# One unit later: where the compressed keys' scores, softmax and turn stand in the first attention

## The reference

```python
sc = jnp.einsum('bgrqd,bgnd->bgrqn', qq, kc_h).astype(jnp.float32) * scale
valid = cmp_end[None, :] <= t[:, None]
p_c = jax.nn.softmax(jnp.where(valid, sc, NEG), axis=-1) * valid
o_c = jnp.einsum('bgrqn,bgnd->bgrqd', p_c.astype(vc_h.dtype), vc_h)
...
p_s = jax.nn.softmax(ss, axis=-1).reshape(b, g_n, r_n, QUERY_BLOCK, top, SEL_BLOCK)
o_s = jnp.einsum('bgrqkc,bgqkcd->bgrqd', p_s.astype(v_sel.dtype), v_sel)
...
p_w = jax.nn.softmax(jnp.where(m_w, sw, NEG), axis=-1)
o_w = jnp.einsum('bgrqk,bgkd->bgrqd', p_w.astype(vwb.dtype), vwb)
return gg[..., 0:1] * o_c + gg[..., 1:2] * o_s + gg[..., 2:3] * o_w
```

## Time and profile before

| what | us |
|---|---|
| median of 3 runs | 1531.16 (1530.28 to 1531.87) |
| the profiled execution's own time | 1531.69 |
| its span | 1529.9 |
| PE busy in the span | 1505.9 (98%) |
| DVE busy | 1203.9 (79%) |
| ACT busy | 1015.9 (66%) |
| chain that ended last: PE's share | 81% |

### The profile page before, as it was taken

How to read it: one execution, slowest core, us unless ns; L and a number is a source line. 1 busy time by engine, 2 the same in 40 slices (tenths; PEclk the granted TensorE clock), 3 DMA queues, 4 the chain that set the end, 5 groups by cost and what they waited for, 6 DMA issues and landing times.

```text
span 1529.9 us, 29802 instructions
## 1 busy us (share of the span) xinstructions
PE 1505.9 (98%) x12684; PEld 1400.1 (92%) x12684; DVE 1203.9 (79%) x1702; ACT 1015.9 (66%) x1566; POOL 8.3 (1%) x18
## 2 busy tenths in 40 slices
PE   9999999999999999999999999999999998999998
PEld 9999999988889999999988889969999897899997
DVE  7999766889758799667898768876898578688864
ACT  7786865667646776765676546685777467677753
POOL 0000000000000000000000000000000001000000
PEclk9999999999999999999999999999999999999999
DMA  7522135555554422244655546402555543255551
GB/s 291 193 95 102 57 138 193 205 183 193 207 178 158 158 98 85 84 165 166 233 191 184 214 170 241 165 1 87 218 193 193 191 142 136 84 208 182 191 193 55
DMA packets 35700, 245.55 MB, mean 161 GB/s; under 512 B 4208, under 2 KB 4592, under 8 KB 6512
## 3 DMA queue, kind: packets, MB, share of 16 engines
q1 hardware_dynamic: 35568, 243.65, 44.5%
HBM read 242.58 MB, written 1.05 MB: 159 GB/s over the span
## 4 chain that ended last, share of the span: by engine, by line
PE 81%; DVE 11%; ACT 5%; DMA 1%; issue 1%; SPq 0%; DVEq 0%; ACTq 0%
PE PS L420 81%; DVE WL L1982 2%; DVE SB L1991 1%; DVE SB L1982 1%; DVE SA L1982 1%; ACT SB L1232 1%; DMA RAW<-w_in 1%; ACT WH L1235 1%; ACT SB L1909 1%; DVE SB L2260 1%; DVE SB L1986 1%; ACT SB L1235 1%; PE PS L423 0%; DVE SA L1991 0%; DVE SA L2162 0%
## 5 line engine op out<-in xcount | busy, mean ns | idle before, releaser
L420 PE MATMUL PS<-XHL,WH 128*128 128x256 f32 (+2 forms) x4080 | 847.9, 301 | 4.6 <-ACT SA L1410 2.8
L420 PEld LDWEIGHTS PS<-XHL,WH 128*128 128x128 f32 (+1 forms) x4080 | 645.8, 187 | 41.4 <-issue 5.9
L420 PE MATMUL PS<-XHL,WL 128*128 128x256 f32 (+1 forms) x2392 | 670.0, 280 | 0.0
L1235 ACT CAST WH<-RAW 128x2048 fp32r<-128x2048 f32 (+1 forms) x235 | 427.3, 1822 | 267.3 <-PE PS L420 255.4
L1982 DVE TENSOR_TENSOR WL<-RAW,WH 128x2048 fp32r<-128x2048 f32 (+1 forms) x235 | 512.0, 2181 | 109.2 <-ACT WH L1235 108.8
L420 PEld LDWEIGHTS PS<-XHL,WL 128*128 128x128 f32 (+1 forms) x2392 | 448.8, 188 | 0.4
L420 PE MATMUL PS<-INHL,WH 128*128 128x512 f32 (+1 forms) x1216 | 334.2, 343 | 0.0
L420 PE MATMUL PS<-INHL,WL 128*128 128x256 f32 x960 | 270.0, 281 | 0.0
L420 PEld LDWEIGHTS PS<-INHL,WH 128*128 128x128 f32 x1216 | 210.1, 188 | 27.6
L420 PEld LDWEIGHTS PS<-INHL,WL 128*128 128x128 f32 x960 | 181.2, 189 | 0.0
L1982 DVE TENSOR_TENSOR SB<-SB 128x510 f32<-128x510 f32 (+3 forms) x171 | 112.6, 660 | 14.8 <-ACT SB L1232 11.4
(11 more groups left out here) (156 smaller groups left out, 1436.7 us busy)
## 6 DMA issues: line engine op xcount, KB each, us to landing
RAW<-w_in SPq DMA_DIRECT2D x51, 1024.0 KB, 4.8
RAW<-w_up SPq DMA_DIRECT2D x44, 1024.0 KB, 4.8
RAW<-f_in SPq DMA_DIRECT2D x44, 1024.0 KB, 4.8
RAW<-w_down SPq DMA_DIRECT2D x22, 1024.0 KB, 4.8
RAW<-f_out SPq DMA_DIRECT2D x22, 1024.0 KB, 4.8
RAW<-a_w_in SPq DMA_DIRECT2D x10, 1024.0 KB, 4.9
RAW<-w_out SPq DMA_DIRECT2D x8, 1024.0 KB, 4.7
RAW<-w_bdn SPq DMA_DIRECT2D x4, 1024.0 KB, 4.8
```

The source lines that it names most:

```text
L420: return e.matmul(out, l, r, start=start, stop=stop, skip_group_check=True)
L1235: e.copy(out, x).then_inc(*A.up(*key, of=of))
```

## The change

In all three engines one number goes up by one. `cmp_scores` moves from u = 1 to u = 2, behind the second value chunk and ahead of `turn(0)`. DVE's `cmp_soft` and ACT's exponential move from u = 2 to u = 3, `cmp_turn` and the copy from u = 3 to u = 4. `compressed(0)` stays at the end of `av(1)` at u = 4. No instruction is added or taken away. The banks of PSUM are handed out in another order, since the compressed scores take theirs later.

```diff
@@ tensor @@
                             ps.give(st, "v", u - 1)
-                        if u == 1:
+                        if u == 2:
                             cmp_scores()
                     if 0 <= u - 2 < 16:
                         turn(u - 2)
-                    if u == 3:
+                    if u == 4:
                         cmp_turn()
                     if u < 16:
                         for r in range(2):
                             ps.give(st, "sc", u, r)
-                        if u == 2:
+                        if u == 3:
                             ps.give(st, "cs")
```

## The result

The changed kernel takes 1535.72 us (median of 8 runs, 1535.18 to 1536.76), the kernel before in the same comparison 1531.45 (8 runs, 1530.05 to 1534.05). The ratio is 1.0028, with a 95% interval of 1.0019 to 1.0038: 4.3 us slower. The forecast was 1534.0 with a range of 1532.0 to 1536.3.

What follows compares the result with a forecast made beforehand. PE, busy 98% of the span, was taken as the bound. 1531.69 + 1.6 (new waits of 4.7 less 2.8 removed, within 0.3) + 1.0 for the clock gave 1534.3, adjusted towards the median to 1534.0; range 1532.0 to 1536.3.

Steps and rivals of the forecast that it cites:

- forecast case: New PE waits for DVE plus a clock fall: 1534.0 us, own range 1533.0 to 1535.7, chance 0.55.
- The value chunk at the full clock: Second value chunk, now behind dense matmuls, runs at 2.4 GHz: 5.78 us in place of 6.89, 1.11 less.
- running clock: Step-by-step timeline from 982.16 with lengths from before, putting scores(5) at 1004.1, 1.6 us later than before.
- The waits that go: PE's 0.79 us wait inside turn(1), for values(1), and a mask's 0.47 us wait for PcT's bank disappear.
- The waits that come: PE waits 2.0 us ahead of turn(2), 2.0 ahead of cmp_turn, both for DVE, and 0.7 at compressed(0) for PcT.
- The clock: Low clock moves behind the compressed scores' new place or the waits; likeliest cost 1.0 us, between 0 and 3.4.
- 1.11 + 0.41 us: Time expected saved at full clock: 1.11 in the second value chunk, 0.41 in the mask and scores(2).
- waits alone: Rival: the new waits come but the clock holds; 1533.3 us, by the median 1532.8; chance 0.28.
- A clock that stays low: Rival: the clock falls and stays low over several stretches; 1537.4 us; chance 0.10.
- No change: Rival: before's clock falls in other executions too or not at all, covering the added waits; 1531.2 us; chance 0.02.
- faster rival: DVE's parts are shorter than measured beside 306 GB/s transfers, so PE waits less; down to 1528.4 us; chance 0.05.

Runs made afterwards that it cites:

- e4: Changed kernel with the 16 compressed-score matmuls spread, two at a time, among the first 24 of the second value chunk; stretch 30.37 us, ratio to before 1.0031.
- e9: Changed kernel with the edits of both e4 and e6, scores spread and waits filled; stretch 29.27 us, ratio to before 1.0016.
- e6: Changed kernel with 12 unread matmuls added ahead of turn(2) and 15 ahead of cmp_turn; stretch 30.35 us, ratio to before 1.0019.
- e3: Changed kernel with only cmp_soft(0) moved ahead of tops(3) on DVE; stretch 27.50 us, ratio to before 1.0013.
- e8: Kernel before with only ACT's weight chunk moved from ahead of values(1) to behind the units; stretch 25.46 us, second profile 26.68, ratio to before 0.9997.
- e1: Kernel before with only the compressed weights' transposes and their copy PcT one unit later; stretch 28.11 us, ratio to before 1.0006.
- e2: Changed kernel with the compressed scores back behind the first value chunk; softmax, transposes and copy stay later; stretch 31.83 us, ratio to before 1.0030.
- e5: Kernel before with the compressed scores spread, two at a time, among the first 24 matmuls of the second value chunk; stretch 26.03 us, ratio to before 0.9994.

## Why the prediction was right, and where its size was off

The measured time lies in the range, 1.7 us above the forecast, and the mechanism is that of the forecast case: new waits for DVE and a fall of the clock. The likelier outcome did not come, though: 1535.72 is above the 1534.2 from which the prediction counted a result as slower, and it gave that 0.36, and 0.61 to a change too small to see. The range held with some luck. The forecast case's own range ended at 1535.7; the 1536.3 is 2.3 us above the forecast, while one more stretch of 3.4 us at half clock costs at most half of it, 1.7, and would have ended the range at 1535.7; the sum behind the 1536.3 is not given. Step by step:

- **The value chunk at the full clock**: 989.35 - 983.6 = 5.75 us against 5.78 worked out, and the compressed scores start at 989.35, where the running clock, shifted by the 0.44 us by which this execution was late already, has them at 989.3. Right, but the change does not buy it in each execution: the second profile of before has the chunk at the full clock too.
- **The waits that go**: those for `values(1)` and for PcT's bank are gone. Right. (The first depends on the scores standing alone behind the value chunk: with spread scores, in e4 and e9, it is back with 0.57 us.)
- **The waits that come**: 2.0, 2.0 and 0.7 us were forecast. PE stood still from the end of `scores(4)` to 1000.45 for 1.66 us, and again for 1.88. The third did not show in the changed kernel, since the low clock had covered it; in e6 and e9 it is 0.39. Without any fall the changed order takes 29.27 us, the order of before 25.95: 3.3 us. The forecast had 1.6 against a before with a fall, which is 1.6 + 1.54 = 3.1. Right to 0.2.
- **The clock**: this is the term that was mis-sized. I took 1.0 us, a fall half hidden in the waits. There were two falls in both profiles; taken singly they cost 1.08 and 1.10 us, together 2.24 and 2.47. The first lengthened `scores(3)`, with which DVE's chain begins, and so counted in full; the second struck `av(1)` and `compressed(0)`, behind the waits, where PE is the bound again. With 2.2 in place of 1.0 the sum from the profiled execution is 1531.69 + 1.6 + 2.2 = 1535.5; that execution itself took 1536.14.
- **The comparison**: I took the fall in before as part of that kernel. The second profile has none. The kernel before takes 25.95 or 27.49, the changed one 31.5 to 31.7; so the difference is 4.0 to 5.8 us by the profiles, and 4.3 by the timed runs. How often before has its fall, two profiles cannot tell. The 1.11 + 0.41 us that I booked as removed are thus gained only in executions with that fall. Counted from an execution without it, the same working gives 1.5 us more.
- **The rivals**: waits alone is out, by e9, which shows what that would have been. A clock that stays low did not come; it rose again after each fall. No change is out, but its premise, that the clock does not fall in other executions of before, came true. DVE's parts were as long as before: from `cmp_soft(0)` at 997.17 to `tops(4)` at 1002.75 it took 5.58 us, where I had 1.94 + 1.28 + 2.45 = 5.67. So the faster rival is out. Its reason rests on a misread row: the 306 GB/s belong to 986.1 to 989.5, ahead of `cmp_soft(0)`. From 989.9 to 991.9, under it, the DMA moved 74 GB/s, from 993.3 to 995.9 145, in the changed kernel 0 under both parts, and they took 1.94 and 2.44 us there where they had taken 1.94 and 2.45.

The Trainium skill (TensorE: Matmul & The Clock Gate, HAM oscillation) says that matmul bursts parted by long waits start at half rate. For the second fall the traces agree: it stood behind waits of 1.66 and 1.88 us, and e6 and e9, with the waits filled, have none. In e3 one such wait of 1.88 us brought no fall. The first fall stands behind the compressed scores, in which PE did not wait. The price in the Terms of the same page of the Trainium skill, half of the time at half rate, makes an estimate of 1.7 us for the 3.4 us of before; the two profiles give 1.54.

What stays open: why the lone scores brought a fall in one profile each of before and e8, in both of the changed kernel, in e1, e2 and e6, and none in e3 and in the other profile each of before and e8.

## What to carry to other kernels

Work that is off the path because it lies under a long piece of another engine loses its cover when it is moved behind that piece: count what stands behind it in its own queue, and who waits for that. Moving the consumer's place in one queue (three instructions on an idle DVE, in e3) gave back 1.77 of the 3.3 us that the move costs in waits. A stretch of narrow matmuls or of waits can have a second price, the clock of the dense work behind it: 1.08 to 1.54 us here, in most profiles and not in all. Spread among wide matmuls, as in e5, the narrow ones cost only their own time. And before a difference of a microsecond or two between two profiles is put down to an edit, see whether both have the same falls, and take a second profile of each.

## What the runs showed that I had not expected

The same program has the low clock in one execution and not in another, at the same instructions: 27.49 and 25.95 us for the kernel before, 26.68 and 25.46 for e8. Filling two waits with 27 matmuls whose result nobody reads made the changed order 1.16 us faster in the stretch. And neither fall hid: where PE had slack of 1.7 us behind it, the first still cost 1.08, since the work that it slowed fed another engine's chain.
